# The middle tap of a three-tap convolution, moved from VectorE to ScalarE for the latent queries and keys

## The reference

```python
def dwconv_centered(x, w):          # depthwise, 3 taps, zero padding at both ends
    ...

def even_proj(xm, w_in, conv_qk, b_igate, b_fgate):
    proj = xm @ w_in
    q, k, v, o, z_m, gates, u_p, z_p = jnp.split(proj, EVEN_SPLITS, axis=-1)
    qk = jax.nn.silu(dwconv_centered(jnp.concatenate([q, k], -1), conv_qk))
    q, k = jnp.split(qk, 2, axis=-1)
    ...
```

## Time and profile before

| What | Value |
|---|---|
| median of 3 runs | 2673.61 us (2669.53 to 2678.39) |
| profiled execution | 2674.96 us, its span 2673.1 us, mean granted clock 0.894 |
| busy, share of the span | PE 1946.9 us (73%), DVE 1980.9 (74%), ACT 568.1 (21%), POOL 1047.9 (39%) |
| chain that ended last, by engine | PE 40%, DMA 23%, POOL 17%, DVE 14%, issue 4%, ACT 1% |
| L2223, the middle tap | 24 instructions, 476 to 484 ns, first at 1007.5, last at 1907.5 us |

### The profile page before, as it was taken

The page is one execution under the profiler, slowest core; times in us unless marked ns, Lnnn a source line. Parts: engine busy times, 40 slices in busy tenths (PEclk is TensorE's granted clock), DMA queues, the critical chain, the costliest instruction groups (busy, mean ns, idle before and its releaser), DMA issues.

```text
span 2673.1 us, 20832 instructions
## 1 busy us (share of the span) xinstructions
PE 1946.9 (73%) x7688; PEld 1337.6 (50%) x7688; DVE 1980.9 (74%) x2458; ACT 568.1 (21%) x854; POOL 1047.9 (39%) x645
## 2 busy tenths in 40 slices
PE   8999999698005777777775000039999999899997
PEld 5877558547002222222222000039788888688885
DVE  6787796987995766544445999999865689777666
ACT  2053010100000000100001000023434444544343
POOL 0000003464685456454555888840065640000000
PEclk9999999899558999999999555569999999999998
DMA  9663878999999999999999999988943458687552
GB/s 374 257 252 126 314 283 344 409 421 421 417 422 422 421 421 421 421 421 422 422 421 422 421 422 422 422 325 303 363 157 136 159 201 350 260 298 289 199 204 95
DMA packets 123509, 887.60 MB, mean 332 GB/s; under 512 B 13841, under 2 KB 14353, under 8 KB 16529
## 3 DMA queue, kind: packets, MB, share of 16 engines
q0 software_dynamic: 80208, 584.09, 52.9%
q1 hardware_dynamic: 39456, 279.73, 28.2%
q10 hardware_dynamic: 3744, 22.47, 2.1%
HBM read 884.13 MB, written 2.10 MB: 332 GB/s over the span
## 4 chain that ended last, share of the span: by engine, by line
PE 40%; DMA 23%; POOL 17%; DVE 14%; issue 4%; ACT 1%; ACTq 0%; DVEq 0%; SPq 0%
PE psum L818 23%; POOL W L686 10%; DMA W<-in_peer_v,W 9%; POOL early_rows L686 7%; DMA W<-in_peer_u,W 5%; DMA early_rows<-in_peer_v,W 5%; PE psum L774 3%; PE psum L750 3%; DMA early_rows<-in_peer_u,W 3%; PE psum L936 3%; PE psum L1090 2%; DVE split L1875 1%; DVE W L2208 1%; PE psum L906 1%; DVE early_rows L2208 1%
## 5 line engine op out<-in xcount | busy, mean ns | idle before, releaser
L818 PE MATMUL psum<-split,hi 128*128 128x512 f32 x1664 | 515.9, 391 | 7.7 <-DVE split L1875 4.5
L2208 DVE CUSTOM_DVE_ANT_0 W<-W,XN 128x2048 f32<-128x2048 f32 x145 | 329.5, 2291 | 202.6 <-DMA W<-in_peer_u,W 201.3
L1090 PE MATMUL psum<-W,HT 128*128 128x512 f32 x616 | 287.0, 610 | 256.7 <-ACT HT L1527 158.1
L1324 ACT ACTIVATE split<-ring 128x1024 fp32r<-128x1024 f32 x272 | 283.6, 1059 | 709.3 <-PE psum L818 302.4
L2208 DVE CUSTOM_DVE_ANT_0 early_rows<-early_rows,XN 128x2048 f32<-128x2048 f32 x111 | 251.9, 2291 | 134.6 <-DMA early_rows<-in_peer_u,W 133.8
L818 PEld LDWEIGHTS psum<-split,hi 128*128 128x128 f32 x1664 | 312.3, 188 | 73.9 <-issue 8.4
L686 POOL DMA_INDIRECT W<-in_peer_v,W x155 | 280.4, 1809 | 168.3 <-PE psum L1090 140.6
L1875 DVE TENSOR_TENSOR split<-ring,split 128x1024 fp32r<-128x1024 f32 x206 | 247.4, 1225 | 127.9 <-ACT split L1324 126.8
L1090 PEld LDWEIGHTS psum<-W,HT 128*128 128x128 f32 x616 | 112.6, 192 | 430.7 <-issue 285.8
L686 POOL DMA_INDIRECT W<-in_peer_u,W x145 | 204.9, 1413 | 174.0 <-DVE W L2208 83.2
L710 POOL TENSOR_TENSOR split<-ring,split 128x1024 fp32r<-128x1024 f32 x66 | 168.6, 2580 | 225.9 <-ACT split L1324 225.9
(11 more groups left out here) (364 smaller groups left out, 3167.9 us busy)
## 6 DMA issues: line engine op xcount, KB each, us to landing
ring<-in_ada SPq DMA_DIRECT2D x51, 1024.0 KB, 5.5
ring<-in_odd SPq DMA_DIRECT2D x48, 1024.0 KB, 5.5
XN<-in_ada POOLq DMA_DIRECT2D x21, 1024.0 KB, 7.9
ring<-in_w_out SPq DMA_DIRECT2D x16, 1024.0 KB, 6.9
ring<-in_pq SPq DMA_DIRECT2D x16, 1024.0 KB, 9.2
ring<-in_c_v SPq DMA_DIRECT2D x16, 1024.0 KB, 7.8
ring<-in_c_k SPq DMA_DIRECT2D x16, 1024.0 KB, 8.0
ring<-in_w_even SPq DMA_DIRECT2D x16, 1024.0 KB, 6.4
```

Source lines behind the costliest of these rows:

```text
L818: m = nc.tensor.matmul(dst, lhs, rhs, start=(k == 0 and b == 0 and not (features and i % 2)), stop=(k == KD - 1 and b == 2 and not (featur ...
L1090: m = nc.tensor.matmul(o[c], DIAG[j % DIAGS], row[:, 512 * c:512 * c + 512], start=(j == 0), stop=(j == P - 1))
L1324: A(split[:, 2048 * (n % PIECES):2048 * (n % PIECES) + 1024], ring[:, at:at + 1024], ACT.Copy)\
L2208: V.tensor_tensor_reduce(out=row, in0=row, in1=xn3[:, tt, :], scale=1.0, scalar=0.0, op0=ALU.mult, op1=ALU.add, accum_out=PACT[:, c:c + 1])\
```

## The change

The middle tap of the latents' queries and keys is made by ScalarE: a new `conv_middle` copies a group of 128 channels out of PSUM with the tap's column as scale. It stands between the hi pieces 3 and 4 of the chunk that follows, four groups at a time. VectorE's `conv_unit` then has only its two neighbour taps, and waits until ScalarE has made both groups of the bank. The context's keys (`c_k`) keep the three operations.

```diff
+            def conv_middle(name, c, dst, c0):
+
+                for i in range(4 * c, 4 * c + 4):
+                    if i % 2 == 0:
+                        wait_unit(act, (name, i // 2))
+                    A(dst[:, i, :], bank((name, i // 2))[:, S * (i % 2):S * (i % 2) + S], ACT.Copy,
+                      scale=column("conv_qk", 16 + c0 + i)).then_inc(sem("conv_middle"), 1)
...
-            latent_hi("l_q", 1)
-            latent_hi("l_k", 0)
+            latent_hi("l_q", 1, lambda _: conv_middle("l_q", 0, QL2, 0))
+            latent_hi("l_k", 0, lambda _: conv_middle("l_q", 1, QL2, 0))
             conv_silu(QL2, 16)
-            latent_hi("l_k", 1)
+            latent_hi("l_k", 1, lambda _: conv_middle("l_k", 0, KL2, 8))
             latent_hi("l_g", 0)
-            latent_hi("l_v", 0)
+            latent_hi("l_v", 0, lambda _: conv_middle("l_k", 1, KL2, 8))
...
                 x_, y = bank(key)[:, S * half:S * half + S], dst[:, i, :]
-                seq(TS(y, x_, column("conv_qk", 16 + c0 + i), None, ALU.mult))
+                if name in ("l_q", "l_k"):
+
+                    dve.wait_ge(sem("conv_middle"), c0 + i - i % 2 + 2)
+                else:
+                    seq(TS(y, x_, column("conv_qk", 16 + c0 + i), None, ALU.mult))
                 seq(STT(y[:, 1:S], x_[:, 0:S - 1], column("conv_qk", c0 + i), y[:, 1:S], ALU.mult, ALU.add))
                 m = STT(y[:, 0:S - 1], x_[:, 1:S], column("conv_qk", 32 + c0 + i), y[:, 0:S - 1], ALU.mult, ALU.add)
```

## The result

The changed kernel takes 2677.59 us (median of 20 runs, 2672.94 to 2681.99) beside 2673.95 us for the kernel before (20 runs, 2669.53 to 2678.43): ratio 1.0015, interval 1.0009 to 1.0022. That is 3.6 us slower, inside the 0.3% that counts as no change here, but a loss and no gain. The forecast was 2676 us (2675.9 by its sum), its range 2667 to 2684, and "within 0.3%" with a chance of 0.85.

What follows compares the result with a forecast made beforehand. VectorE was taken as full around the edit (6.1 us per slot against TensorE's 5.8). The later `in_c_v` load's +2.3 us on the profiled 2674.96 us gave 2677.3; that execution lies 1.35 above the median, so 2675.9, range 2667 to 2684.

Steps and rivals of the forecast that it cites:

- VectorE's wait: VectorE idle for ScalarE before the first STT of the four chunks, about 3.4, 3.3, 1.3 and 5.2 us.
- The rule behind it: In each chunk VectorE waits until start of hi piece 3 + 0.95 + 0.84 (two copies) + 0.04 us.
- TensorE's stalls: TensorE waits 0.6 to 1.1 us at the third piece of three chunks, about 2 us in (l_v,0).
- The load's landing: The `in_c_v` load ending the chain takes 5.1 us, between bounds 4.79 and 7.91, and lands +2.3 us later.
- Rival 2: Slower: the load released by lo piece 3 of (l_v,0) still takes 7.91 us, +5.1, or +6 to +8; chance 0.25.
- The mis-sized term: The `in_c_v` load behind lo piece 3 of (l_v,0) goes out at about 1900.4 instead of 1895.29.
- The clock's loss: TensorE's 1.7 us lost to its clock in (l_v,1) is kept, as the new pause is 2.5 us.
- a drop behind the stall in (l_v,0): A fall of TensorE's clock behind its 2.0 us stall in (l_v,0) would lie in TensorE's slack.
- the rest of the trace is the old one, shifted: Behind (l_v,1)'s start, no stage behind 1920 changes its length by more than the clock's 1.7 us.
- Rival 1, the relief counts: Faster: TENSOR_SCALARs off the chain give 2.6 us and the clock 1.7, -4.3 us, to 2669.3; chance 0.15.

Runs made afterwards that it cites:

- changed_scans: Changed kernel with VectorE's scans of the gate rows put ahead of its wait for the last values; one run, 2672.91 us.
- copies_twice: Changed kernel with four more ScalarE copies of the same size, into an unread buffer, behind each group of copies; one run, 2678.41 us.
- not_lv: Changed kernel with copies and waits kept only in (l_q,1), (l_k,0) and (l_k,1), and (l_v,0) as before; one run, 2674.72 us.
- lv_only: Changed kernel with the copies and the wait kept in (l_v,0) alone, the other three chunks as before; one run, 2681.97 us.
- wait_only: Changed kernel, copies and waits kept, but VectorE makes its TENSOR_SCALAR again; 2684.82 us, 1.0043 of the kernel before.
- relief_only: Kernel before without the 16 TENSOR_SCALAR of the middle tap, without copies and waits; 2668.14 us, 0.998 of the kernel before.
- second_bank: Changed kernel with only each chunk's second bank (8 of 16 taps) handed to ScalarE; 2670.02 us, 0.9989 of the kernel before.
- silu_later: Kernel before with gate-row scans ahead of VectorE's last-values wait and the keys' Silu behind the first two hi pieces of (l_v,1); 2667.12 us, 0.9982.
- best: Kernel before with the two moves of silu_later and the hand-over of second_bank; 2666.70 us, 0.9981 of the kernel before.

## Why the prediction was right, step by step

- *VectorE's wait* was forecast at 3.4, 3.3, 1.3 and 5.2 us, and was 3.50, 3.65, 1.27 and 4.61, put down to ScalarE each time. The rule behind it (start of hi piece 3 + 0.95 + 0.84 + 0.04) held: 1806.67 is 1.89 behind the 1804.78 of the chain, by the rule 1.83. The first STTs came 2.09, 3.10, 2.37 and 5.99 us later, forecast 2.03, 2.7, 1.9 and 5.1. The copies took 454 to 484 ns, forecast 474.
- *TensorE's stalls*: forecast 0.6 to 1.1 us in three chunks and 2 in the fourth; found 0.76, 0.76, 0.87 and 2.40.
- *The load's landing*, the term without a row, was taken as 5.1 us between 4.79 and 7.91; it was 5.12. That it fits so closely is luck: behind the same wait of VectorE, the same load took 5.26 us in `changed_scans` and 5.92 in `copies_twice`. Rival 2 rested on the far end and fell with it, though its other part, the lateness of the issue, was partly right.
- *The mis-sized term is that issue*: +6.0 us instead of +5.1. The delays ahead of it were each a little larger than worked out: hi piece 3 of (l_k,0) +1.0 for +0.65, the hi pieces of (l_k,1) +1.5 for +1.1, the landing of 1891.51 +1.2 for +0.4. They are carried from chunk to chunk by TensorE's stalls, and `not_lv` measured what they come to, +1.7 us at A. With +6.0 - 2.8 the load is used at +3.2, and A is +3.19, forecast +2.3.
- *The clock's loss* was expected to stay, since a wait of 2.4 us had been enough for it elsewhere; the pause was 1.86 instead of 2.5 us and the loss went. (That a drop behind the stall in (l_v,0) would lie in TensorE's slack was not put to the test by the change, whose clock stayed at 1.00; in `lv_only` and `wait_only` it fell there, and TensorE stood on the chain.) The step was wrong by 1.5 us, and so was the one behind it, that "the rest of the trace is the old one, shifted": the stretch between (l_v,1) and (l_u,1) grew by the same 1.5 us, as GpSimd's pieces and the scans set its end. The two cancelled; the forecast owes that to luck.
- *Rival 1, the relief counts*, asked the right question. It is worth 4.5 us at A by `relief_only`. That this is near its 4.3 is luck: of the 4.3, 2.6 were VectorE's and 1.7 the clock's, which lies behind A. VectorE's part was larger, 4.5, and at B only 3.1 us were left, although the clock's loss in (l_v,1) was gone (22.06 us). And it is there only where the hand-over is free, as in part of `second_bank`. The advice of the Trainium skill (Perfetto Trace Analysis, Optimizing Scalar/DVE Operations), to offload a saturated DVE to Scalar, holds for the work and says nothing of the place: the same trace that bears out the cheap copy (0.47 us) shows 13.0 us of VectorE's waits for it.

The median moved by 3.6 us and the profile's B by 3.2, for a forecast of +2.3, which lies just under the interval (1.0009 is +2.4 us).

## What to carry to other kernels

Work that is moved from a full engine to an idle one is paid at the hand-over: look up what stands ahead of it in the idle engine's queue, and when the full engine arrives. Here ScalarE had the room and the copies cost next to nothing by themselves, but they stood behind a piece that waited for a load or for TensorE, and VectorE arrived up to 4.6 us earlier; handing over only the units for which it comes later turned the loss into a small gain. And a gain on the chain (here the clock's 1.5 us) counts only if the next thing that the chain joins isn't already set by another engine.

## What the runs showed of the hardware that I had not expected

- VectorE's small operations on 8 partitions with two operands in SBUF go at GpSimd's pace while it works on pieces of 128x1024: a scan of 8x256 takes 2.75 us for 0.73, a TENSOR_TENSOR of 8x512 2.71 for 0.68. The step of GpSimd's pieces is 20.90/8 = 2.6 us, so by my estimate VectorE gets in about one instruction per piece, and it shows as busy all the while. The Trainium skill (SBUF — State Buffer, Who interferes with whom) has the rule: a DVE instruction with two SBUF inputs contends with a GpSimd instruction that reads SBUF, and what they share is an exclusive lock. The traces agree as to VectorE, by 2.71 beside 0.68 us for the TENSOR_TENSOR; that a lock does it no run here shows. I had not applied it to the stretch behind the change.
- Loads of `in_c_v` of 1 MB on the chain took from 5.12 us (after, behind VectorE's wait) to 9.10 (in `silu_later`) from issue to use; what sets this was not isolated.
- What TensorE loses to its clock behind the pause ahead of (l_v,1) is not ordered by the pause: 3.7 us of it cost 1.7 us before; 3.1 in `second_bank` and 2.7 in `copies_twice` cost 3.0 and 3.1 (24.78 and 24.95 us for the 96 matmuls); 2.9 in `not_lv` and 1.9 after cost 0.2 (22.02 and 22.06). The stretch after A in `second_bank`:

```profile
1904.00:1911.00 7.00, 3.91 (x18) 2.90 (x16) 3.29 (x4) 6.96 (x7) 0.00 (x0) 0.93 0.97 370
1911.00:1916.00 5.00, 4.96 (x12) 3.92 (x13) 5.00 (x5) 2.56 (x4) 0.00 (x0) 0.50 0.66 241
```

  It is at 0.50 (1.2 GHz) for 5 us, though the pause was shorter than before. Nor does the wait for the gate rows order what follows: the clock fell to about a half behind 0.64 us (before), 2.14 (after) and 1.24 (`silu_later`), and stayed at 1.00 behind 0.55 (`changed_scans`) and 1.24 (`best`). What decides it these runs don't show. A forecast should keep such a loss of 0 to 3 us as a range of its own.
